# The input projection in three rounded products: one projection of a hybrid decoder step on one core

## What is computed

```python
xn = rmsnorm(x, g_attn_norm)                  # 544 x 1024
z = xn @ w_in                                 # 1024 x 1792; q, k, v, conv (3 parts), memory query
...                                           # attention in a window, short conv, memory attention
h = x + mix @ w_out                           # 1024 x 1024
hn = rmsnorm(h, g_ffn_norm)
y = h + moe(hn, ...)                          # top 4 of 32 experts, clamped SwiGLU
```

## Time and profile before

| | |
|---|---|
| median of 3 runs | 1428.47 us (1428.11 to 1431.58) |
| profiled execution, span | 1427.3 us |
| PE, PEld, DVE, ACT, POOL busy | 1404.2, 1021.3, 1185.9, 991.8, 399.0 us |
| first record of the input projection | 28.39 us |
| first product with `w_out` | 169.50 us |
| first rows of the expert periods on PE | 262.45 us |

### The profile page before, as it was taken

One profiled execution on the slowest core, in us unless ns is written; L12 is line 12 of the kernel. 1 busy time (PEld: TensorE's weight loads), 2 busy tenths in 40 slices (PEclk: granted clock), 3 DMA queues, 4 the chain that ended last, 5 costly groups with the idle time before them and its releaser, 6 DMA issues.

```text
span 1427.3 us, 18390 instructions
## 1 busy us (share of the span) xinstructions
PE 1404.2 (98%) x6675; PEld 1021.3 (72%) x6675; DVE 1185.9 (83%) x1081; ACT 991.8 (69%) x954; POOL 399.0 (28%) x231
## 2 busy tenths in 40 slices
PE   9999999999999999999999999999999999999995
PEld 6876754777777777777777777777777777777773
DVE  3164455899999999999999999999999999999996
ACT  3134422777777777777777777777777777777774
POOL 2012121443555664222222222222222222222203
PEclk9999999899999999999999999999999999999998
DMA  9640065599999999999999999999999999999984
GB/s 367 206 152 16 35 229 217 193 382 355 375 383 372 362 358 353 369 379 384 372 376 367 365 374 358 372 368 366 368 372 366 379 365 362 374 368 372 367 302 147
DMA packets 52260, 461.94 MB, mean 324 GB/s; under 512 B 11369, under 2 KB 15435, under 8 KB 26489
## 3 DMA queue, kind: packets, MB, share of 16 engines
q1 hardware_dynamic: 39641, 437.77, 79.3%
q0 software_dynamic: 10624, 20.42, 6.6%
q10 hardware_dynamic: 1936, 2.99, 0.7%
HBM read 447.41 MB, written 24.31 MB: 331 GB/s over the span
## 4 chain that ended last, share of the span: by engine, by line
PE 94%; DVE 2%; DMA 1%; issue 1%; POOL 1%; ACT 1%; POOLq 0%; SPq 0%; DVEq 0%; ACTq 0%
PE psum L2270 25%; PE psum L2271 25%; PE psum L2272 24%; PE psum L1879 7%; PE psum L2040 4%; PE psum L2283 2%; PE psum L2254 2%; PE psum L2265 2%; PE psum L1849 1%; DMA ring<-in_w_mem_kv 1%; POOL small L761 0%; ACT ring L836 0%; DMA area<-hn_tbl,idx_i 0%; PE psum L1950 0%; PE psum L1974 0%
## 5 line engine op out<-in xcount | busy, mean ns | idle before, releaser
L1608 DVE TENSOR_TENSOR low<-raw,high 128x2048 fp32r<-128x2048 f32 x384 | 865.4, 2284 | 43.3 <-ACT high L1026 42.4
L1026 ACT CAST high<-raw 128x2048 fp32r<-128x2048 f32 x384 | 725.1, 1913 | 91.3 <-PE psum L2272 88.6
L2270 PE MATMUL psum<-high,area_r 128*104 128x512 f32 x1536 | 610.4, 397 | 0.9 <-DVE area_r L1677 0.9
L2271 PE MATMUL psum<-high,area_r 128*104 128x512 f32 x1536 | 603.3, 393 | 0.0
L2272 PE MATMUL psum<-low,area_r 128*104 128x512 f32 x1536 | 602.6, 392 | 0.0
L2272 PEld LDWEIGHTS psum<-low,area_r 128*104 128x104 f32 x1536 | 257.6, 168 | 97.1
L2270 PEld LDWEIGHTS psum<-high,area_r 128*104 128x104 f32 x1536 | 257.8, 168 | 91.7 <-DVE area_r L1677 1.3
L2271 PEld LDWEIGHTS psum<-high,area_r 128*104 128x104 f32 x1536 | 258.2, 168 | 90.3
L679 POOL DMA_INDIRECT area<-hn_tbl,idx_i x32 | 158.4, 4949 | 95.0 <-DVE idx_i L1575 72.3
L644 POOL CAST pick_r<-area 64x104 fp32r (+1 forms) x33 | 30.4, 921 | 460.8 <-PE psum L2272 460.6
L692 POOL DMA_INDIRECT y_tbl<-area,idx_i x31 | 61.7, 1991 | 222.4 <-ACT area L1036 199.7
(11 more groups left out here) (261 smaller groups left out, 901.7 us busy)
## 6 DMA issues: line engine op xcount, KB each, us to landing
raw<-in_w_gate_up SPq DMA_DIRECT2D x128, 2048.0 KB, 10.8
raw<-in_w_down SPq DMA_DIRECT2D x64, 2048.0 KB, 10.4
ring<-in_w_in SPq DMA_DIRECT2D x7, 1024.0 KB, 21.1
area<-in_w_out SPq DMA_DIRECT2D x1, 4096.0 KB, 30.4
ring<-in_w_mem_kv SPq DMA_DIRECT2D x2, 1024.0 KB, 9.4
area<-in_x_prompt SPq DMA_DIRECT2D x4, 512.0 KB, 11.7
ring<-in_mem_kT SPq DMA_DIRECT2D x1, 2048.0 KB, 10.1
ring<-in_cache_mem_v SPq DMA_DIRECT2D x1, 2048.0 KB, 8.3
```

What stands on the lines that cost most here:

```text
L1026: nc.scalar.copy(high_w(i), raw_w(t)).then_inc(sem("w_high"), 1)
L1608: v.tensor_tensor(low_w(t), raw_w(t), high_w(i), ALU.subtract).then_inc(sem("w_low"), 1)
L2270: mm(bank, high, wh, start=start, stop=False)
L2271: mm(bank, low, wh, start=False, stop=False)
```

## The change

The input projection is made as the experts' products are: the transposed rows are split once into `xh` and `xl` (`x_split` on ACT, `x_low` on DVE), every tile of weights into `wh` and `wl` (`w_split` on ACT, `w_low` on DVE), and each float32 matmul becomes three fp32r matmuls. The row tiles are loaded into the place of the late weight chunks of `w_in`, which are now loaded after the rows' transposes, and `w_out` is loaded tile by tile to other places, seven of its eight tiles near the end of the attention; the scaling of `wo` moves with it. `hnr` and `hnT` move as well. The biases are loaded and split ahead of the first tiles instead of behind the fifth. Chunks 3 and 4 of the first expert are loaded at another point of SP's program.

```diff
@@ sync
+            for c in range(2):
+                load_wi(c)
+            for g in range(3):
+                sp.dma_start(bias_raw[g * NE:(g + 1) * NE], biases).then_inc(sem("ld_b"), 16)
...
             sp.wait_ge(sem("xT_pe"), 14)
-            sp.dma_start(wo, w_out.rearrange("(k p) n -> p k n", p=P)).then_inc(sem("ld_wo"), 16)
+            for c in range(4, 7):
+                load_wi(c)
+            load_wo(7, 8)
...
+            sp.wait_ge(sem("job_pe"), JB[MEM_UNIT - 1])
+            sp.wait_ge(sem("z_pe"), 24)
+            load_wo(0, 3)
+            sp.wait_ge(sem("job_pe"), JB[MEM_UNIT] - 1)
+            load_wo(3, 7)
...
-                    for q in range(4):
+                    for q in range(3):
                         load_chunk(0, q)
-                if j == NTT - 2:
-                    sp.wait_ge(sem("h_part"), 6 * j + 4)
+                if j == NTT - 1:
+                    sp.wait_ge(sem("group_pe"), 2)
+                    load_chunk(0, 3)
                     load_chunk(0, 4)
@@ scalar
+            def x_split(r):
+                cols = slice((r - 2) * P, (r - 2) * P + row_tile(r)[1])
+                ac.wait_ge(sem("xT_ready"), 2 * r + 2)
+                nc.scalar.copy(xh[:, :, cols], xT0[:, :, cols]).then_inc(sem("xh_ready"), 1)
+            def w_split(i):
+                if i % 2 == 0:
+                    ac.wait_ge(sem(ld_wi(i // 2)), 16 if i < 8 else 32)
+                if i >= 3:
+                    ac.wait_ge(sem("z_pe"), 2 * i - 4)
+                nc.scalar.copy(wh_z[i % 3], wi[i // 2][:, :, (i % 2) * P:(i % 2 + 1) * P]).then_inc(sem("wh_ready"), 1)
+            ac.wait_ge(sem("ss_ready"), 7)
+            ac.wait_ge(sem("mkv_pe"), 1)
+            w_split(0)
+            x_split(2)
+            x_split(3)
             mem_out(0)
...
+            x_split(4)
+            x_split(5)
+            x_split(6)
+            w_split(1)
             mem_out(1)
+            ac.wait_ge(sem("ld_b"), 64)
...
+            ac.wait_ge(sem("bias_low"), 1)
+            w_split(2)
@@ scalar, z_odd
                 nc.scalar.copy(z_out(t, 1), banks[7][:, 0:HALF]).then_inc(sem("z_act"), 1)
+                if i + 3 < NZ:
+                    w_split(i + 3)
@@ vector
+            def x_low(r):
+                cols = slice((r - 2) * P, (r - 2) * P + row_tile(r)[1])
+                dv.wait_ge(sem("xh_ready"), r - 1)
+                v.tensor_tensor(xl[:, :, cols], xT0[:, :, cols], xh[:, :, cols], ALU.subtract).then_inc(sem("xl_ready"), 1)
+            def w_low(i):
+                dv.wait_ge(sem("wh_ready"), i + 1)
+                v.tensor_tensor(wl_z[i], wi[i // 2][:, :, (i % 2) * P:(i % 2 + 1) * P], wh_z[i % 3], ALU.subtract).then_inc(sem("wl_ready"), 1)
...
+            dv.wait_ge(sem("bias_high"), 1)
...
@@ vector, z_even
                 v.tensor_copy(z_out(t, 0), banks[6][:, 0:HALF]).then_inc(sem("z_dve"), 1)
+                if i + 2 < NZ:
+                    w_low(i + 2)
...
             z_even(4)
             conv_gate(0)
+            for t in range(3):
+                gain(t)
...
             z_even(5)
             conv_gate(1)
+            for t in range(3, 7):
+                gain(t)
...
+            for par, n in ((0, 3), (1, 2)):
+                dv.wait_ge(sem(f"st_hn{par}"), 16 * n)
             link(v.tensor_copy(cnt, banks[0][:, 160:192]))
@@ tensor, z_half
+                if half == 0:
+                    pe.wait_ge(sem("wl_ready"), i + 1)
                 wait(pe, "z_act" if half else "z_dve", i)
                 for k in range(KD):
-                    last = mm(banks[6 + half][:, 0:HALF], wi[i // 2][:, k, (i % 2) * P:(i % 2 + 1) * P],
-                              xT0[:, k, half * HALF:(half + 1) * HALF], start=(k == 0), stop=(k == KD - 1))
+                    mm(bank, wh[:, k, :], xh[:, k, cols], start=(k == 0), stop=False)
+                    mm(bank, wh[:, k, :], xl[:, k, cols], start=False, stop=False)
+                    last = mm(bank, wl[:, k, :], xh[:, k, cols], start=False, stop=(k == KD - 1))
@@ tensor
-            pe.wait_ge(sem("xT_ready"), 10)
+            pe.wait_ge(sem("xl_ready"), 3)
             z_half(8, 0)
+            pe.wait_ge(sem("xl_ready"), 5)
+            z_half(8, 1)
             mem_keys()
```

More of the change, by code:

```diff
@@ L142, in build @@
             raw_b = [over.enter_context(nc.sbuf_tensor(f"raw{q}", [P, CHW], F32)) for q in range(NCH)]
+        with ExitStack() as over:
+            for q in range(2):
+                over.enter_context(nc.sbuf_tensor(f"under{q}", [P, CHW], F32))
+            over.enter_context(nc.sbuf_tensor("under2", [P, 9280 - 2 * CHW], F32))
+            xl_t = over.enter_context(nc.sbuf_tensor("xl", [P, KD * NT], F32R))
+            over.enter_context(nc.sbuf_tensor("under3", [P, 2 * D], F32))
+            wh_t = over.enter_context(nc.sbuf_tensor("wh", [P, D], F32R))
         low_b = [sb(f"low{q}", CHW, F32R) for q in range(NCH)]
@@ L202, in build @@
         assert W_OFF + 14 * D == NBUF * CHW
+        xh, xl = view(area_r, 0, [KD, NT]), view(xl_t, 0, [KD, NT])
+        wh_z = [view(area_r, KD * NT, [KD, P]), view(area_r, KD * NT + D, [KD, P]), view(wh_t, 0, [KD, P])]
+        wl_c = [(low_b[4], HW), (low_b[5], 0), (low_b[5], HW)] + [(t, 0) for t in high_b]
+        wl_z = [view(t, off, [KD, 256])[:, :, h * P:(h + 1) * P] for t, off in wl_c for h in range(2)]
         mckT = view(ring, W_OFF, [2, NB, 256])
@@ L295, in build, with ld_x, ld_wi, ld_wo @@
         banks = [psum[:, i * 512:(i + 1) * 512] for i in range(8)]
+        def ld_x(j):
+            return ("ld_x0_wi4", "ld_x1_wi5", "ld_x2_wi6", "ld_x3_wo0", "ld_x4_wo3")[j]
+        def ld_wi(c):
+            return f"ld_wi{c}" if c < 4 else ld_x(c - 4)
+        def ld_wo(t):
+            return "ld_wo7" if t == 7 else ld_x(3 if t == 0 else 4)
         def bias_bank(j, half):
@@ L424, in load_chunk, with load_wo @@
                 sp.dma_start(raw_b[q][:, :], src).then_inc(sem(f"chunk{q}"), 16)
+            def load_wo(first, last):
+                for t in range(first, last):
+                    sp.dma_start(wo[t], w_out[t * P:(t + 1) * P, :]).then_inc(sem(ld_wo(first)), 16)
             sp.wait_ge(sem("xT_pe"), 14)
-            sp.dma_start(wo, w_out.rearrange("(k p) n -> p k n", p=P)).then_inc(sem("ld_wo"), 16)
+            for c in range(4, 7):
+                load_wi(c)
+            load_wo(7, 8)
             sp.wait_ge(sem("mkv_ready"), 2)
@@ L794, in _ @@
                 ap, n = row_tile(r)
-                ac.wait_ge(sem(f"ld_mem{r}" if r < 2 else f"ld_x{r - 2}"), 16)
+                ac.wait_ge(sem(f"ld_mem{r}" if r < 2 else ld_x(r - 2)), 16)
                 wait(ac, "ss_ready", r)
@@ L1217, in _ @@
                 rows_T(r)
-            for r in range(2, 9):
-                if r < 7:
-                    ms(r)
-                if 3 <= r < 7:
+            for r in range(2, 7):
+                ms(r)
+                if r >= 3:
                     norm(r - 1)
-                if r == 6:
-                    norm(6)
-                if r >= 4:
-                    rows_T(r - 2)
+                if r == 4:
+                    rows_T(2)
+                if r == 5:
+                    rows_T(3)
+            norm(6)
+            w_low(0)
+            x_low(2)
+            rows_T(4)
+            x_low(3)
+            rows_T(5)
+            x_low(4)
+            rows_T(6)
+            x_low(5)
+            x_low(6)
+            w_low(1)
+            dv.wait_ge(sem("bias_high"), 1)
+            v.tensor_tensor(bias_r[2 * NE:3 * NE, 2 * D:3 * D], bias_raw[2 * NE:3 * NE, 2 * D:3 * D],
+                            bias_r[2 * NE:3 * NE, 2 * D:3 * D], ALU.subtract)
+            v.tensor_tensor(bias_r[NE:2 * NE, 0:2 * D], bias_raw[NE:2 * NE, 0:2 * D], bias_r[NE:2 * NE, 0:2 * D],
+                            ALU.subtract).then_inc(sem("bias_low"), 1)
             def z_even(t):
@@ L1472, in _ @@
             z_even(7)
-            for t in range(2, 5):
-                gain(t)
             denominators(1, 0)
@@ L1480, in _ @@
             z_even(9)
-            gain(5)
             denominators(2, 0)
@@ L1486, in _ @@
             z_even(11)
-            gain(6)
-            gain(7)
             denominators(3, 0)
@@ L1858, in _ @@
             mem_kv(1, 0)
-            mem_kv(0, 1)
             rows_T(2)
             rows_T(3)
+            mem_kv(0, 1)
+            rows_T(4)
+            rows_T(5)
+            rows_T(6)
             mem_kv(1, 1)
-            for r in (4, 5, 6):
-                rows_T(r)
             def mem_keys():
@@ L2039, in part @@
                 for t in tiles:
-                    last = mm(bank[0:n, :], zT[:, t, j * P:j * P + n], wo[:, t, half * 512:(half + 1) * 512],
+                    last = mm(bank[0:n, :], zT[:, t, j * P:j * P + n], wo[t][:, half * 512:(half + 1) * 512],
                               start=(t == tiles[0]), stop=(t == tiles[-1]))
@@ L2064, in group_part @@
                     for g in range(4):
```

(2 more changed lines are left out.)

50 lines of the change are left out of this document (20 added, 30 removed).

## The result

| | before | changed |
|---|---|---|
| median | 1428.86 us (1428.11 to 1431.58, 6 runs) | 1434.16 us (1433.69 to 1436.27, 6 runs) |
| profiled execution, span | 1427.3 us | 1432.2 us |
| first record of the projection | 28.39 | 33.48 |
| first product with `w_out` | 169.50 | 167.16 |
| last `hn` store, issued and landed | 253.26, 255.2 | 251.02, 258.9 |

The ratio is 1.0035, with a 95% interval from 1.0024 to 1.0046: 5.3 us slower, where 0.7 us faster was forecast. The time lies in the prediction's range of 1418.5 to 1437 us, but above 1432.8, up to which the prediction would have called it the same, and on the slow side.

The account below looks back on a forecast made before the run. The prediction took PE to bound the kernel, with 94% of the chain. From 1427.3 us it took 8.1 of lead, added 5.8 at the end and 1.6 for the clock, then 1.2 from span to median: 1427.8 us, range 1418.5 to 1437.

Parts of the forecast that it names:

- the lead of 8.1 us at the first product with `w_out`: End of the attention: the first product with `w_out` comes at about 161.4 instead of 169.50 us.
- The clock, "in the range only": PE at the start: new waits at 25 to 28 and 39 to 42 us may cost slow-clock pieces; not in the sum.
- The pace: Projection on PE: a half tile of 24 fp32r matmuls takes 2.94 us instead of 3.67, gaining 20.4 us over 28.
- The start: First tiles: projection starts 3.9 us later, the bias split makes PE wait 3.6 and 0.6; together 8.1 us.
- The waits in the attention: PE waits for the DVE and ACT loop: 2.5 us third unit, 0.7 fourth, 1.7 for the `w_out` gains.
- The end: Last stores: the final hn store lands behind two chunks in SP's queue, so gather and first transposes come 5.8 us later.
- The clock at the end: First expert products: PE runs at 1.2 GHz for 3 us after standing still; 1.6 us taken, bounds 0 and 3.5.
- The end costs nothing: Rival at the last stores: small stores overtake or chunks land sooner, 1420.4 us; chance 0.26 shared with a faster pace.
- Slower products: Rival in the projection: a fixed cost per matmul, 1431.2 us at 0.130 us a step, 1435.4 at 0.140; chance 0.15.
- Loads and streams don't overlap: Rival in the projection: weight load and stream add up, 4.99 us per half tile, about 1480 us; chance 0.04.
- DVE and ACT set the pace: Rival in the nine later projection tiles: PE's gain of 13.1 us shrinks to about 7, result 1434; chance 0.10.
- the two signs that would have shown the prediction wrong: Projection and last stores: a half tile over 3.2 us, or the last store landing within 3 us.

Follow-up runs that it names:

- e1: The changed kernel with chunks 3 and 4 issued behind the fifth tile's hn store instead of ahead of it; ratio 1.0039.
- e13: The changed kernel with three and two filling matmuls of 512 float32 columns in PE's two waits of the start; ratio 1.0018.
- e14: The changed kernel itself, unaltered, measured beside e13 as its base; ratio 1.0041.
- e11: The changed kernel with seven and five filling matmuls of 512 float32 columns in PE's two waits of the start; ratio 1.0044.
- e6: The changed kernel with each projection matmul of 272 columns made as two of 136, each weight block loaded twice; 1489.93 us, a single run.
- e5: The changed kernel with chunks 3 and 4 issued only behind the gather of the first expert's rows; 1427.91 us, ratio 0.9992.
- e2: The kernel before with only chunks 3 and 4 moved to where the change issues them, ahead of the fifth tile's stores; 1435.71 us, ratio 1.0036.
- e10: e9 with the last four matmuls of the memory product put ahead of the sixth row tile's transposes; 1420.90 us, ratio 0.9944.
- e12: e10 with five filling matmuls of 512 float32 columns in PE's wait ahead of the projection; 1422.47 us, ratio 0.9947.
- e7: The changed kernel with the bias split later and the ACT weight split of three tiles behind the second half of the exponentials; ratio 0.9990.
- e9: The changed kernel with the edits of e5 and e7 together; 1422.47 us, ratio 0.9945.

## Why the prediction was wrong

**The failed step: the lead of 8.1 us at the first product with `w_out`, above all because the pieces at 1.2 GHz behind the new waits stood in it at nothing.** The lead was 2.3, 5.8 us less. By its own steps:

- *The clock, "in the range only".* I wrote that the new waits at 25 to 28 and 39 to 42 us may cost a piece at 1.2 GHz, and left it out of the sum, while the same waits stood in the sum as idle time. Both pieces came, and a third behind the third unit's wait. The first two cost 2.4 us (e1 against the changed kernel) to 3.0 (e13 against e14). The third cost 1.3 to 1.5, by the time from this unit to the `w_out` product with it (57.17 to 57.39 us) and without it (55.86). Together that is 3.7 to 4.5 of the 5.8 us. They do not come in every execution: e1 has neither of the first two, e11 not the third.
- *The pace.* 3.00 us a half tile, not 2.94: 28 x 0.06 = 1.7 us. I took the stream in proportion from 512 columns. A step is 0.230 us at 512 columns, 0.125 at 272 and 0.112 at 136 (e6): a floor per matmul lies right under this stream, and my 0.093, from a stream of one column in float32, was too low for it.
- *The start.* With the clock full the projection would have started at 31.6 (e1 and e13), 0.7 before my 32.3; with the piece, at 33.5. The wait behind the biases was 2.2 us, not 3.6 + 0.6; PE came to it later here, but with the full clock in e1 it was 2.8, so I had it too long. The second tile started at 42.70, forecast 42.2, and at 41.45 in e1.
- *The waits in the attention*: forecast 2.5 in the third unit, 0.7 in the fourth, 1.7 for the gains; found 2.6 + 0.6, 0.4 and 1.6. The sum is 4.9 forecast and 5.2 found.

These overlap (a pace costs less where a wait follows), and I can't split them more finely. In e1, where only the third piece came, the `w_out` product still was 3.4 us later than forecast, which the pace and that piece nearly fill; but it had also entered the second tile 0.75 us ahead of my forecast, so that 1 us or so stays without a place.

**The end was right.** 5.8 us forecast, 5.6 found (-5.9 in the way back with e5, 4.4 in the kernel before with e2). I had the cause as the order in SP's queue. e1 shows that order alone is not it, since the gather on another queue suffers the same when it is the one behind. Had the change been forecast as "store first", the same method would have gone wrong.

**The clock at the end stays open.** I expected 3 us at 1.2 GHz from the first rows on; in the changed kernel it was 5. The stretch from the first rows to the end was 1164.9 us in the one profiled execution of before. It was 1166.0 to 1166.3 in the three later ones with the full clock at their first expert products (e5, e10, e12), and 1166.1 to 1168.4 in all others. So the 1.5 us that agree with my 1.6 aren't shown to be the clock: that agreement may be luck, since the executions with the full clock lie nearly as far above before.

**The rivals.** "The end costs nothing" is out by e2 and e5. "Slower products" is right in kind and small: 0.125 us a step. "Loads and streams don't overlap" is out by the step of 0.125 with a load of 0.19 in the records. "DVE and ACT set the pace" gave nearly the measured time, 1434, for a reason that PE's 97.63 busy us of 102 refute. The mechanism that decided, PE's own clock behind the waits that the change makes, was a sentence at the end of a range and no rival. Neither of the two signs that would have shown the prediction wrong (a half tile over 3.2 us, the last store within 3 us) came, since both looked at terms that held in the main. The chances also count the cases of the first two rivals as faster and slower throughout, though two of their own times, 1424.4 and 1431.2, lie in the stretch that the prediction calls the same.

## What to carry to other kernels

Count a new wait of TensorE twice: as idle time, and as a possible piece of the work behind it at half speed. Here waits of 1.8 to 3.1 us cost another 1.2 to 1.7 us each in most executions of the changed kernel and nothing in others, so such a piece belongs into the sum with its chance, and one profile isn't enough to say that an edit made it or took it away. Before dividing a stage into matmuls of fewer columns per load of weights, check how far its stream lies above the shortest step. And bulk loads placed ahead of a chain of small dependent transfers (store, gather) belong behind the last of them, not between them.

## What the hardware showed that I had not expected

- A matmul in fp32r with a load of 128x128 weights takes 0.112 us with 136 columns and 0.125 with 272 (0.230 with 512 columns and 128x104 weights, rows 6): nearly flat below 272, nearly in proportion above.
- A gather of 104 rows on POOL's queue took 12.3 us instead of 5.0 until its rows were on PE, with two chunks of 2 MB in SP's queue ahead of it: separate queues did not shield it.
- TensorE dropped to 1.2 GHz behind waits of 2.2, 2.6 and 3.1 us in the changed kernel, but not behind 2.8 and 3.1 us at the same places of the same code in e1, nor behind 2.6 us in e11. Behind a wait of 1.8 us in the third unit it dropped in e12 and not in e7, e9 and e10. The length of the wait alone does not decide; what does, these runs don't show.
